# Hybrid attention decoder step: a bias store issued later, four products reordered, operand sums ahead of their splits, and a count of its own for a weight quarter

## The reference, cut to what matters

```
shift, scale, gate = split(c @ ada_w + ada_b, 3)
h = rmsnorm(x, norm_g) * (1 + scale) + shift
q, 6 x kv, gts, hc, bc, cc, z = split(h @ w_in)          # the projection
k_cmp = silu(blocks(kc) @ w1_k) @ w2_k ; v_cmp likewise   # the compression
o_attn = gated sum of compressed, selected and window attention,
         each with a bias by distance: tab[t5_bucket(dist)]
y_conv = bc * causal_conv3(cc * hc)
out = rmsnorm(x + gate * (concat(o_attn * silu(z_a), y_conv * silu(z_c)) @ w_out), final_g)
```

## Time and profile before

| | |
|---|---|
| median of 3 runs | 1537.35 us (1535.48 to 1538.67) |
| the profiled execution | 1532.23 us |
| its span, first to last instruction | 1530.4 us |
| PE, DVE, ACT busy | 1433.0, 964.0, 704.4 us |
| mean granted TensorE clock | 0.979 |

### The profile page before, as it was taken

One profiled execution on the slowest core, in us unless ns is written; L12 is line 12 of the kernel. 1 busy time (PEld: TensorE's weight loads), 2 busy tenths in 40 slices (PEclk: granted clock), 3 DMA queues, 4 the chain that ended last, 5 costly groups with the idle time before them and its releaser, 6 DMA issues.

```text
span 1530.4 us, 27904 instructions
## 1 busy us (share of the span) xinstructions
PE 1433.0 (94%) x10526; PEld 1236.4 (81%) x10526; DVE 964.0 (63%) x2312; ACT 704.4 (46%) x1546; POOL 234.7 (15%) x441
## 2 busy tenths in 40 slices
PE   5987998999999999969989999999999999999998
PEld 2876998999999999957767777777777766788886
DVE  2643768787787887848666666667567654653226
ACT  2421232423323223226567777777777765631111
POOL 1100010101101011031021242232222131000000
PEclk9998999999999999989999999999999999999999
DMA  9376123423333334297321141121121129963231
GB/s 345 99 137 126 28 84 90 117 60 96 86 75 105 78 90 112 62 316 237 111 91 43 29 108 56 43 70 47 33 57 30 30 74 357 265 207 98 82 98 35
DMA packets 169669, 164.76 MB, mean 108 GB/s; under 512 B 53644, under 2 KB 150028, under 8 KB 164160
## 3 DMA queue, kind: packets, MB, share of 16 engines
q1 hardware_dynamic: 153904, 94.11, 22.6%
q0 software_dynamic: 15632, 68.87, 14.9%
HBM read 131.27 MB, written 35.83 MB: 109 GB/s over the span
## 4 chain that ended last, share of the span: by engine, by line
PE 80%; DVE 7%; DMA 5%; ACT 3%; issue 3%; SPq 1%; DVEq 0%; POOL 0%; ACTq 0%
PE PS L1258 26%; PE PS L1619 11%; PE PS L1425 8%; PE PS L1390 7%; PE PS L1369 5%; PE PS L1307 4%; PE PS L1370 3%; PE PS L1472 2%; PE PS L1214 1%; DMA gw<-in_ada_w 1%; PE PS L1215 1%; PE PS L1216 1%; DMA adaw<-in_ada_w 1%; PE PS L1576 1%; DMA wr<-in_w_in 1%
## 5 line engine op out<-in xcount | busy, mean ns | idle before, releaser
L1258 PE MATMUL PS<-bo,wsl 128*128 128x264 f32 x4104 | 504.5, 286 | 11.1 <-DVE qp L2186 5.8
L1258 PEld LDWEIGHTS PS<-bo,wsl 128*128 128x128 f32 x4104 | 503.6, 190 | 12.2 <-DVE qp L2186 6.0
L1882 ACT ACTIVATE pr<-PS,nm 128x640 f32<-128x640 f32 (+7 forms) x256 | 181.0, 708 | 45.2 <-DVE nm L2392 42.6
L1715 ACT ACTIVATE wsl<-wsum 128x512 fp32r<-128x512 f32 x105 | 65.6, 630 | 231.9 <-DVE wsum L2107 231.9
L1905 ACT ACTIVATE ptt<-PS 128x512 f32<-128x512 f32 x264 | 149.6, 601 | 41.6 <-PE PS L1390 41.4
L1390 PE MATMUL PS<-ident,pr 128*128 128x128 f32 x1056 | 147.2, 274 | 0.0
L1425 PE MATMUL PS<-ptt,kvt 128*64 128x256 f32 x1056 | 136.7, 390 | 0.0
L1390 PEld LDWEIGHTS PS<-ident,pr 128*128 128x128 f32 x1056 | 122.4, 141 | 8.9 <-ACT ptt L1905 0.4
L1425 PEld LDWEIGHTS PS<-ptt,kvt 128*64 128x64 f32 x1056 | 66.9, 136 | 41.2 <-issue 16.5
L2392 DVE CUSTOM_DVE_ANT_0 PS<-PS,near,nm 128x256 f32<-128x256 f32 x192 | 94.7, 493 | 6.8
L2391 DVE TENSOR_REDUCE nm<-PS 128x1 f32<-128x128 f32 (+5 forms) x128 | 70.5, 551 | 39.2 <-PE PS L1370 38.7
(11 more groups left out here) (358 smaller groups left out, 2403.2 us busy)
## 6 DMA issues: line engine op xcount, KB each, us to landing
wr<-in_w_in SPq DMA_DIRECT2D x32, 512.0 KB, 5.6
adaw<-in_ada_w SPq DMA_DIRECT2D x8, 1024.0 KB, 9.5
wr<-in_w_in SPq DMA_DIRECT2D x32, 256.0 KB, 4.3
q_stacked<-qp POOLq DMA_DIRECT2D x64, 128.0 KB, 2.7
qb<-q_stacked SPq DMA_DIRECT2D x32, 256.0 KB, 3.1
mr<-mixed SPq DMA_DIRECT2D x16, 512.0 KB, 3.9
mixed<-yy POOLq DMA_DIRECT2D x16, 264.0 KB
xb<-in_x_prompt POOLq DMA_DIRECT2D x8, 512.0 KB, 4.7
```

The source lines that it names most:

```text
L1258: ins = pe.matmul(PS[:, 2 * q + c, 0:H // 2], w[:, x, kk, :], b[:, y, kk, c * H // 2:(c + 1) * H // 2], start=(first and kk == 0 and x == ...
L1882: act.activation(pr[r][:, h, 0:k], score_cols(b0, w), ACT.Exp, scale=-1.0, bias=nm[:, r, h:h + 1], accum_out=rsum[:, r, h:h + 1]).then_inc ...
```

## The change

- The bias store becomes a function that POOL calls in its list of the projection, at (0,1), behind the store of the gates. `rows` now lies in the partitions 64 to 79 of `kvs`, and the waits of ACT and POOL for the store go; SP's wait before the read in attention stays.
- Block 0 runs its first four products in the order 2, 3, 0, 1. PE waits for the last kv copy before (0,1) and for the gate sums before (0,3).
- The pieces are numbered by sum, and adding and splitting have a table each. Up to piece 11 a piece is split one list entry after it is added, behind the next add. Pieces 16 to 19 are added at (1,7) and (2,0) into `ts` and `er`, `eg`, pieces 12 to 15 at (2,1) and (2,2) into `qp` over the kept copy; they are split at (2,3) to (2,6). `whole(O11)` moves from (2,2) to (1,6). The three-add form is gone. The rounding of the queries waits for split 15.
- The first quarter of `w1[0]` counts on `wr_ld`, for which PE waits before the first step; for the other three it waits at step 8. ACT and DVE no longer wait for the prompt's stores at step 4.

```diff
-        rows = sb("rows", [NH, XW], cx=cC)
+        rows = kvs[64:64 + NH, 0:XW]
...
-        PIECE = [(s_, k) for s_ in range(3) for k in range(HK)] + [(3, 2), (3, 3), (4, 2), (4, 3), (3, 0), (3, 1), (4, 0), (4, 1)]
-        PIECES = {(0, 0): 0, (0, 1): 1, (0, 2): 2, (0, 3): 3, (0, 4): 4, (0, 5): 5, (0, 6): 6, (0, 7): 7, (1, 0): 8, (1, 4): 9,
-                  (1, 5): 10, (1, 6): 11, (2, 2): 12, (2, 3): 13, (2, 4): 14, (2, 5): 15, (2, 6): 16, (2, 7): 17, (3, 0): 18, (3, 1): 19}
+        PIECE = [(s_, k) for s_ in range(5) for k in range(HK)]
+        ADDED = {(0, 0): (0,), (0, 1): (1,), (0, 2): (2,), (0, 3): (3,), (0, 4): (4,), (0, 5): (5,), (0, 6): (6,), (0, 7): (7,),
+                 (1, 0): (8,), (1, 1): (9,), (1, 4): (10,), (1, 5): (11,), (1, 7): (16, 17), (2, 0): (18, 19), (2, 1): (12, 13), (2, 2): (14, 15)}
+        SPLIT = {(0, 1): (0,), (0, 2): (1,), (0, 3): (2,), (0, 4): (3,), (0, 5): (4,), (0, 6): (5,), (0, 7): (6,), (1, 0): (7,),
+                 (1, 1): (8,), (1, 4): (9,), (1, 5): (10,), (1, 6): (11,), (2, 3): (12, 13), (2, 4): (14, 15), (2, 5): (16, 17), (2, 6): (18, 19)}
+        def op_sum32(x):
+            if x < 12:
+                return (er if x % 2 else ts[0])[:, :]
+            return f32(qp[:, x - 12, :]) if x < 16 else (ts[1], eg, ts[0], er)[x - 16][:, :]
...
-            load_w1(0, 0)
+            load_w1(0, 0, wr_ld)
...
-            po.wait_ge(tb_ev, 1)
-            rv = rows[:, :]
-            po.dma_start(rowd, ...).then_inc(row_st, 16)
+            def store_bias():
+                rv = rows
+                po.dma_start(rowd, ...).then_inc(row_st, 16)
...
+                    if n == 0 and i == 1:
+                        store_bias()
...
-            pe.wait_ge(kv_ev, 2 * NTT)
             pe.wait_ge(h_ev, NTT)
...
-            pe.wait_ge(ada_ev, 8)
-                        k, op, out = PLAIN[i]
+                        k, op, out = PLAIN[(2, 3, 0, 1)[i] if n == 0 and i < 4 else i]
+                        if n == 0 and i == 1:
+                            pe.wait_ge(kv_ev, 2 * NTT)
+                        if n == 0 and i == 3:
+                            pe.wait_ge(ada_ev, 8)
...
-            pe.wait_ge(xp_ld[2], 64)
+            pe.wait_ge(wr_ld, raw_landed(NBLK - 1) + 16)
             for m in range(32):
+                if m == 8:
+                    pe.wait_ge(xp_ld[2], 48)
...
-                    act.wait_ge(op_sum, 16 if half else 18)
+                    act.wait_ge(op_lo, 16)
...
-                    act.wait_ge(row_st, 16)
...
-                        act.wait_ge(out_st, prompt_out[0])
...
-                    if (n, i) in PIECES:
-                        x = PIECES[n, i]
-                        if x:
-                            op_low(x - 1)
-                        if x == 12:
-                            whole(O11)
+                    for x in ADDED.get((n, i), ()):
                         op_add(x)
-                    if n == NPLAIN and i == 2:
-                        op_low(19)
+                    for x in SPLIT.get((n, i), ()):
+                        op_low(x)
+                    if n == 1 and i == 6:
+                        whole(O11)
...
-                        dve.wait_ge(out_st, prompt_out[0])
```

More of the change, by code:

```diff
@@ L368, in build @@
             sem(n) for n in ("q5_rdy nbn_rdy t5 ev5 ev5d pick_mm pick_rdy e5c s5_mm s5_ev m5 e5 b5_rd o5_mm o5_cp ot_t mix5_rdy mix5_st kn_t kn_ev".split()))
-        wo_ld = list(zip(xp_ld + q_ld, [192, 192, 64, 64] + [128] * 4))
+        wo_ld = list(zip(xp_ld + q_ld, [192, 192, 48, 64] + [128] * 4))
         mr_ld = [sem(f"mr_ld{i}") for i in range(2)]
@@ L583, in summed_at, with sum_ready @@
             return tuple(m for m in prepared_at(n, i) if is_sum(m))
-        PIECE = [(s_, k) for s_ in range(3) for k in range(HK)] + [(3, 2), (3, 3), (4, 2), (4, 3), (3, 0), (3, 1), (4, 0), (4, 1)]
-        PIECES = {(0, 0): 0, (0, 1): 1, (0, 2): 2, (0, 3): 3, (0, 4): 4, (0, 5): 5, (0, 6): 6, (0, 7): 7, (1, 0): 8, (1, 4): 9,
-                  (1, 5): 10, (1, 6): 11, (2, 2): 12, (2, 3): 13, (2, 4): 14, (2, 5): 15, (2, 6): 16, (2, 7): 17, (3, 0): 18, (3, 1): 19}
-        def op_scratch(x):
-            return (er, eg) if x % 2 else ts
+        PIECE = [(s_, k) for s_ in range(5) for k in range(HK)]
[3 more added lines that the diff above has]
+                 (1, 1): (8,), (1, 4): (9,), (1, 5): (10,), (1, 6): (11,), (2, 3): (12, 13), (2, 4): (14, 15), (2, 5): (16, 17), (2, 6): (18, 19)}
+        def sum_ready(x):
+            return x + 1 if x < 12 else x + 5 if x < 16 else x - 3
+        def op_sum32(x):
+            if x < 12:
+                return (er if x % 2 else ts[0])[:, :]
+            return f32(qp[:, x - 12, :]) if x < 16 else (ts[1], eg, ts[0], er)[x - 16][:, :]
         ACT_EV = {(0, True): "cc1 cc0", (1, True): "zt1 zt0", (2, True): "za1 qh1 za0 qh0",
@@ L705, in load_w, with load_w1 @@
                         at += w
-            def load_w1(c, q):
+            def load_w1(c, q, landed=None):
                 src = (cmp_w1_k, cmp_w1_v)[c].rearrange("l (t p) c -> p (l t) c", p=P)
-                sp.dma_start(w1[c][:, 8 * q:8 * q + 8, :], src[:, 8 * q:8 * q + 8, :]).then_inc(xp_ld[2 + c], 16)
+                sp.dma_start(w1[c][:, 8 * q:8 * q + 8, :], src[:, 8 * q:8 * q + 8, :]).then_inc(landed or xp_ld[2 + c], 16)
             def load_rows(c, r):
@@ L926, in _ @@
                 po.dma_start(xb[s % 2][0:rows_of(tile_at(s)), :], xp[:, s - 1, :] if s else xs).then_inc(x_ld[s % 2], 16)
-            po.wait_ge(tb_ev, 1)
-            rv = rows[:, :]
-            po.dma_start(rowd, bass.AP(rv.tensor, rv.offset, [list(rv.ap[0]), [0, P], [1, XW]])).then_inc(row_st, 16)
+            def store_bias():
+                rv = rows
+                po.dma_start(rowd, bass.AP(rv.tensor, rv.offset, [list(rv.ap[0]), [0, P], [1, XW]])).then_inc(row_st, 16)
             po.wait_ge(kv_ev, 2 * NTT)
@@ L1031, in _ @@
             po.memset(xp4[1][:, :, :, :], 0.0).then_inc(xz, 1)
-            po.wait_ge(row_st, 16)
             po.wait_ge(g_st, 16)
@@ L1717, in op_high @@
             def op_high(x):
[L1719 to L1724, removed]
+                s_, k = PIECE[x]
+                act.wait_ge(op_sum, sum_ready(x))
+                if x >= 12:
+                    act.wait_ge(*made(2, 3 if x >= 16 else 1))
+                act.activation(bo[SUMS[s_][0]][:, 0, k, :], op_sum32(x), ACT.Copy).then_inc(op_hi, 1)
             def copied_out(dst, src, func=ACT.Copy, scale=1.0):
@@ L1825, in _ @@
                         high(m)
-                    if (n, i) in PIECES:
-                        op_high(PIECES[n, i])
+                    for x in ((ADDED if n < 2 else SPLIT).get((n, i if n < 2 else i + 1), ())):
+                        if (x < 12) == (n < 2):
+                            op_high(x)
                 if n == 4:
@@ L2124, in op_add @@
                 dst, a, b, op = SUMS[s_]
-                t = op_scratch(x)
-                if x >= 2:
+                t, kept = op_sum32(x), f32(qp[:, k, :])
+                if 2 <= x < 12:
                     dve.wait_ge(op_lo, x - 1)
[L2128 to L2136, removed]
+                if x >= 16:
+                    dve.wait_ge(op_lo, 12)
+                dve.wait_ge(op_kept, 1 if x < 12 else 2)
+                if 12 <= x < 16:
+                    dve.wait_ge(op_sum, 16)
+                own, first_, second = (b, kept, f32(bo[b][:, 0, k, :])) if s_ == 4 else (a, f32(bo[a][:, 0, k, :]), kept)
+                link(dve.tensor_tensor(t, first_, second, op))
+                dve.tensor_tensor(t, t, f32(bo[own][:, 1, k, :]), ALU.add).then_inc(op_sum, 1)
             def op_low(x):
-                (s_, k), t = PIECE[x], op_scratch(x)
+                s_, k = PIECE[x]
                 dst = bo[SUMS[s_][0]]
-                dve.wait_ge(op_sum, x + 1)
+                dve.wait_ge(op_sum, sum_ready(x))
                 dve.wait_ge(op_hi, 1 + x + 1)
-                dve.tensor_tensor(dst[:, 1, k, :], t[0][:, :], f32(dst[:, 0, k, :]), ALU.subtract).then_inc(op_lo, 1)
+                dve.tensor_tensor(dst[:, 1, k, :], op_sum32(x), f32(dst[:, 0, k, :]), ALU.subtract).then_inc(op_lo, 1)
             def conv_inputs(n):
```

1 line of the change is left out of this document (removed).

## The result

| | before | after |
|---|---|---|
| median of 4 runs each | 1537.26 us | 1502.74 us |
| the profiled execution | 1532.23 us | 1502.53 us |
| its span | 1530.4 us | 1500.7 us |
| mean granted TensorE clock | 0.979 | 0.986 |

The profiled executions are 29.7 us apart, the sum in the forecast was 32.6. Here is where the 29.7 came from, stage by stage. Each stage is the difference between the two profiles at one landmark, less what the landmark before it had already gained.

A forecast was written before the change was run, and what follows sets the result against it. TensorE was taken as the bound, apart from four large waits. A 13.7, B and C 6.0 and D 12.9 sum to 32.6 us: 1532.2 becomes 1499.6, with 5.1 for the median 1504.8; range 1496 to 1515.

The forecast's parts named there:

- A: Kv stage: moving the bias store out ends the gate-weight wait, 12.3 us and 1.36 of half clock, together 13.7 us.
- B: Projection's start: reordering four products removes the wait for the gate sums, 4.1 us, and 1.7 us of half clock.
- C: Blocks 2 and 3: sums ahead of splits remove the wait before (3,3); with B 15.3 us, 6.0 after the collision.
- The collision: Block 2: the moved store delays the `wr` load to 188.6; TensorE waits 4.3 us, plus 1.7 clock, 2.2 and 1.0.
- Rival 1: Block 2's load shares bandwidth evenly with the store from its issue, landing at 182; total 39.1 us, 1498.2; chance 0.12.
- Rival 2: The moved store takes ten us longer beside a busy VectorE, 1514.8; chance 0.09.
- D: Compression's start: an own count for the first `w1` quarter removes a 12.4 us wait; 11 to 13.5, taken as 12.9.
- Rival 4: Compression's start: D brings 3 us only, if another arrival (gather, row loads) ends the wait; 1514.7; chance 0.05.

The follow-up runs named there:

- halves_old_order: Changed kernel with the bias store cut in two held DMAs as in halves, and block 0's first four products in the old order: 1501.41 us, 0.9768 of before.
- old_order: Changed kernel with the order of block 0's first four products and TensorE's two waits undone: 1500.32 us, 0.9791 of before.
- halves: Changed kernel with the bias store cut in two DMAs, the second at (1,3) behind the landing of block 2's load: 1489.20 us, 0.9717 of before.
- old_sums: Changed kernel with the order of operand sums and splits undone: 1512.27 us, 0.9869 of before.
- both_now: Changed kernel with the bias store cut in two DMAs, both issued at (0,1) one behind the other: 1501.71 us, 0.9786 of before.
- late: Changed kernel with the whole bias store at (1,3), behind the landing of block 2's load: 1503.97 us, 0.9799 of before.
- store_early: Changed kernel with the bias store issued in the kv stage again: 1507.29 us, 0.983 of before.
- filler: The kernel of halves with 28 unread identity transposes between the tail transposes and the compression's first turn: 1489.99 us, 0.9716 of before.
- changed: The changed kernel as it is, run again on the same chip as two other kernels: 1502.16 us, 0.9787 of before.

## Why the prediction was right

**A** came as worked out: cadence of 10.59 us, no gate wait, 13.7 us. The store's move costs nothing in POOL's list.

**B** came as worked out at its place (4.2 us, no half clock at the start), and by itself it is worth 5.7 us (`halves_old_order`); in this kernel it is absorbed (`old_order`). The forecast's chain of waits holds that already, as its stalls are counted from a TensorE that arrives early; it did not say that B alone brings nothing.

**C** was forecast only together with B, 15.3 us where weights come in time. `halves` measured 16.0; less the 5.7 of B that leaves some 10 for C, and undoing it beside the collision cost 11.2 (`old_sums`).

**The collision** was right in place and kind: `wr` 19.5 us after its issue (18 to 21 was said), ACT and DVE idle 10.8 and 10.1 (11 said), TensorE waiting for g1, `zt1`, g0 and the query low part. Its size was put too high up to (3,3) and too low behind:

- The load landed at 171.5, forecast 188.6 - 15.3 = 173.3 in these times. The wait for g1 was 2.08, not 4.3.
- Half clock of 1.7 us was charged behind that wait. The clock stayed at 1.00 in 172 to 187, behind waits of 2.08, 1.47 and 1.76 us.
- From g1 to g0 TensorE waited 1.47 + 1.76 us, where 2.2 was said; then 0.57 for 1.0.
- The forecast counted from start to start, and so counted, each wait costs 0.26 us more than its bracket (the 24 matmuls ahead of one take 3.18 us, not 2.92): 2.35, 3.77 and 0.83 us, together 6.95 where 9.2 was said.
- Not forecast: a wait of 1.01 before (4,0). DVE stood 3.2 us for block 4's load, which landed 10.1 us after its issue at 214.51; in `halves` the same load took 10.4 us and TensorE did not wait.

Up to (3,3) that gave 2.1 us more than forecast, behind it 1.9 less.

**Rival 1,** even sharing, asked for a landing 14 us after the issue, 166 in these times; it was 171.5. The Trainium skill (DMA: Bandwidth & Descriptors, Queues, rings and completion order) has each engine take turns between queues packet by packet. The trace does not show turns of equal worth. The rate stayed at the store's own in 145 to 161 (104 GB/s) and rose to 151 only in 161 to 171, and the first quarter, issued at 152.04, landed 1.2 us after the store. The landing goes by the store's end and not by the issue: the load left at 152.04, at 156.94 (`old_sums`) and at 158.82 (`old_order`), the store had landed at 166.1, 166.3 and 167.5, and the load was complete 5.4 us after that in all three. `both_now` (5.5) and, with block 3's load, `late` (6.5) show the same.

**Rival 2,** a longer store beside a busy VectorE, is out: VectorE was busy 14.4 of 16 us in 145 to 161, and the store took 32.9 us, beside 35.3 and 33.3 (`store_early`) in the kv stage. The box of the Trainium skill (SBUF — State Buffer, on DVE blocking DMA) speaks of GpSimd's writing of descriptors, and only beside a VectorE instruction in a two-port mode, a condition that the prediction left out; this store's issue took POOL 1.06 us, as in the kv stage (1.05), and nothing was seen to hold it.

**D is the term that was mis-sized:** "11 to 13.5, I take 12.9", and it brought 8.9. What failed is that the two turns and the eight steps would run as at 662.7 before, at full clock, with the query stores alone setting step 4. The twelve row loads were issued as before (the last 0.6 us ahead of the tail in both), but the first turn came 4.23 us behind the tail instead of 2.57. From there to step 4 it took 11.8 us, and 8.7 in `filler`, where the clock is full: the first step 3.7 instead of 1.9 us. So 1.7 us went to the later rows and 3.1 to the steps at half clock. The query stores didn't bind: POOL was past its wait for them 9.1 us behind the tail (647.48), and step 4's copies came later. The half clock that I had booked as saved had moved to the next wait. How late the rows land differs between executions of one kernel. The run `changed` shows, in TensorE's timeline:

```profile
638.42 1.03 PE L1296 MATMUL PS<-ident,tail 128*18 128x128 f32 x8 [1.07 <-DVE eg L2223]
641.55 0.30 PE L1310 MATMUL PS<-ident,xp 128*128 128x128 f32 x1 [2.10 <-DMA xp<-in_cmp_pe_k]
...
651.65 1.16 PE L1320 MATMUL PS<-xt,w 128*128 128x273 f32 x4
```

There step 4 is 13.2 us behind the tail: D brought 24.9 - 13.2 = 11.7. In the ten kernels with D and no filler step 4 came 13.1 (`both_now`) to 16.5 us (`store_early`) behind the tail. So 8.4 to 11.8 is its size, and 12.9 was reached in none. The first turn came 2.8 to 4.8 us behind the tail in all twelve kernels that aren't the one before, and 2.57 in the one trace of that; whether the change has a part in this is open. Rival 4 was right in kind, another arrival does hold TensorE there, but not in size.

**The total** was nearer than the sum, and that was luck: of the 32.6 us summed, the change gave 28.1 in the profiles (29.7 less 1.6 of the start). The median of before lies 5.1 us above its profiled execution, that of after 0.2, so the profiled execution of before was faster than each of the three runs shown ahead (1535.48 at least). The forecast added these 5.1 us to the kernel after as well. So 4.5 us too much in the sum were made up by 1.6 of the start and by 4.9 of an offset that the kernel after doesn't have. By medians the gain is 34.5 us, and 34.6 in `changed`, where both kernels ran on one chip. Why these are some 5 us above the traces is open; the medians of the kernel before alone differ by 4.4 us between the three groups (1532.36, 1535.14 and 1536.78).

## What to carry to other kernels

A big DMA that is moved out of one critical wait has to be laid against each load that is issued while it runs. For this store (16 partitions, each copied 128 times, at some 100 GB/s) the price was the rest of its run, not a share of the bandwidth; for stores of another shape no run here shows it. If it fits in no gap between loads, cut it and hold the second part on the landing of the load between; cutting without the hold changes nothing. An edit that makes an engine arrive earlier at a late load is worth nothing until the load is mended: test it with the collision away before it is kept or thrown out.

## What was not expected of the hardware

- A 1 MB load issued 19 us into the store landed 19.5 us later, 5.4 us after the store's end; with the store over it took 7.0 us. The store itself ran at 104 GB/s, while the same DMA engines move 356 GB/s in 640 to 651. SP's issues are held too, for 5.2 and 8.2 us where they take 0.6 and 1.0 in `halves`.
- Half clock does not follow each wait: none behind 2.08, 1.47 and 1.76 us in block 2 (clock 1.00), but 0.50 behind 2.71 us in `old_sums`, 0.66 behind 4.1 in `old_order`, and, at the compression's start, 0.52 behind 2.3 in `halves` and 0.59 behind 1.77 in `old_order` (642.4 to 650). So the length of the wait alone does not decide; what does is not settled here.
- Filling such a wait with idle transposes kept the clock at 1.00 for the next 16 us.
